# Layer one's gated recurrence run beside the 17 tiles of that layer's projection

## What is computed

```python
xn = rms_norm(h, norm_mix_g[layer])
...
proj = xn @ cd_w_in[j]
lru_x, lru_g, m_x, m_o, m_if = split_cols(proj, CD_SIZES)
...
def rglru_group(xb, gate, conv_w, conv_b, gate_w, gate_b, lam):
    ...
    xc = causal_dwconv(xb.astype(F32), conv_w, conv_b)
    xblk = xc.reshape(B, T, LRU_BLOCKS, LRU_BLOCK)
    gates = jnp.einsum('btnd,gnde->gbtne', xblk, gate_w).reshape(2, B, T, LRU_WIDTH) + gate_b[:, None, None, :]
    r_gate = jax.nn.sigmoid(gates[0])
    i_gate = jax.nn.sigmoid(gates[1])
    log_a = -LRU_C * r_gate * jax.nn.softplus(-lam)
    u = jnp.sqrt(-jnp.expm1(2.0 * log_a)) * (i_gate * xc)
    h = linear_recurrence(jnp.exp(log_a), u)
    return h * jax.nn.gelu(gate.astype(F32))
```

## Time and profile before

| | |
|---|---|
| median of 3 runs | 3634.97 us (3629.35 to 3637.94) |
| the profiled execution | 3619.69 us, its span 3617.7 us |
| PE matmul busy | 3265.8 us (90%) |
| DVE busy | 2353.3 us (65%) |
| ACT busy | 1575.7 us (44%) |
| mean granted clock of TensorE | 0.929 |

### The profile page before, as it was taken

The page is one execution under the profiler, slowest core; times in us unless marked ns, Lnnn a source line. Parts: engine busy times, 40 slices in busy tenths (PEclk is TensorE's granted clock), DMA queues, the critical chain, the costliest instruction groups (busy, mean ns, idle before and its releaser), DMA issues.

```text
span 3617.7 us, 42372 instructions
## 1 busy us (share of the span) xinstructions
PE 3265.8 (90%) x15738; PEld 2681.4 (74%) x15738; DVE 2353.3 (65%) x2345; ACT 1575.7 (44%) x1584; POOL 185.4 (5%) x212
## 2 busy tenths in 40 slices
PE   7967988999999858999998697769999999999996
PEld 6757977878788637878787575658888888888884
DVE  4545436467755446457753436458999999999995
ACT  3131214332223144332222214337777777777772
POOL 0000000000000000000000000000111110111110
PEclk9957988999999978999999897769999999999997
DMA  5200003334433202334432220249999999999993
GB/s 180 82 1 1 1 13 91 104 97 151 145 114 105 76 12 82 99 105 146 144 104 91 92 78 1 82 164 351 387 380 388 379 384 384 381 386 378 390 376 137
DMA packets 118820, 638.42 MB, mean 176 GB/s; under 512 B 13416, under 2 KB 13416, under 8 KB 68784
## 3 DMA queue, kind: packets, MB, share of 16 engines
q1 hardware_dynamic: 98592, 560.52, 41.6%
q0 software_dynamic: 20112, 76.24, 7.0%
HBM read 612.07 MB, written 24.64 MB: 176 GB/s over the span
## 4 chain that ended last, share of the span: by engine, by line
PE 73%; DVE 10%; ACT 2%; issue 1%; DMA 1%; DVEq 1%; SPq 0%; ACTq 0%; POOLq 0%
PE banks L328 25%; PE banks L2467 19%; PE banks L2484 9%; PE banks L920 7%; PE banks L341 3%; DVE chunk_split L301 1%; PE banks L2461 1%; PE banks L2452 1%; PE banks L2473 1%; PE banks L578 1%; PE banks L601 1%; PE banks L1793 1%; DVEq L2769 0%; DVE scratch L1002 0%; DVE scratch L389 0%
## 5 line engine op out<-in xcount | busy, mean ns | idle before, releaser
L328 PE MATMUL banks<-x_scratch,chunk_split 128*128 128x512 f32 x3648 | 845.9, 393 | 36.3 <-DVE x_scratch L315 22.7
L328 PEld LDWEIGHTS banks<-x_scratch,chunk_split 128*128 128x128 f32 x3648 | 686.9, 189 | 189.4 <-issue 46.7
L295 ACT CAST chunk_split<-weight_ring 128x1024 fp32r<-128x1024 f32 x292 | 306.2, 1049 | 987.9 <-PE banks L328 739.9
L2467 PE MATMUL banks<-pair_split,rows 128*128 128x512 f32 x3072 | 710.0, 392 | 0.0
L2467 PEld LDWEIGHTS banks<-pair_split,rows 128*128 128x128 f32 x3072 | 578.6, 188 | 126.5
L301 DVE TENSOR_TENSOR chunk_split<-weight_ring,chunk_split 128x1024 fp32r<-128x1024 f32 x292 | 357.0, 1223 | 227.5 <-ACT chunk_split L295 219.3
L2484 PE MATMUL banks<-pair_split,hidden_t 128*128 128x512 f32 x1536 | 361.4, 394 | 6.1 <-DVE hidden_t L2579 6.1
L2484 PEld LDWEIGHTS banks<-pair_split,hidden_t 128*128 128x128 f32 x1536 | 285.5, 189 | 69.1 <-issue 6.3
L2246 DVE TENSOR_TENSOR pair_split<-mixed,pair_split 128x2048 fp32r<-128x2048 f32 x128 | 293.0, 2290 | 34.5 <-ACT pair_split L2241 34.5
L2246 DVE TENSOR_TENSOR pair_split<-scratch,pair_split 128x2048 fp32r<-128x2048 f32 x128 | 290.4, 2288 | 36.8 <-ACT pair_split L2241 36.7
L2246 DVE TENSOR_TENSOR pair_split<-weight_ring,pair_split 128x2048 fp32r<-128x2048 f32 x128 | 290.3, 2289 | 36.1 <-ACT pair_split L2241 36.1
(11 more groups left out here) (576 smaller groups left out, 3925.3 us busy)
## 6 DMA issues: line engine op xcount, KB each, us to landing
weight_ring<-in_weights SPq DMA_DIRECT2D x292, 512.0 KB, 3.6
mixed<-in_w SPq DMA_DIRECT2D x128, 1024.0 KB, 8.9
weight_ring<-in_w SPq DMA_DIRECT2D x128, 1024.0 KB, 7.6
scratch<-in_w SPq DMA_DIRECT2D x128, 1024.0 KB, 8.7
mixed<-in_w_ada POOLq DMA_DIRECT2D x48, 512.0 KB, 3.8
token_sums<-tables POOLq DMA_DIRECT2D x1, 2560.0 KB, 21.6
residual<-in_x POOLq DMA_DIRECT2D x4, 512.0 KB, 10.0
projected<-in_mem POOLq DMA_DIRECT2D x2, 1024.0 KB, 5.2
```

The lines of the kernel that those rows point to most:

```text
L295: act.copy(chunk_split[:, 0, at:at + KB * P], flat(ring[:, n % RING])).then_inc(chunk_hi.sem, 1)
L328: mm = pe.matmul(lin.bank(j), chunk_split[:, a, at + k * P:at + (k + 1) * P], lin.split[b][k][:, 0:lin.tokens], start=(k, a, b) == (0, 0, ...
L2467: mm = pe.matmul(banks[:, n, :], rows[:, a, k, :], pair_split[k % SLOTS][:, b, n * T:(n + 1) * T], start=False, stop=(k, a) == (KB - 1, 1))
```

## The change

The stage `rg_lru` is gone. Its work is written as a class, `RgLru`, whose three functions are generators: each `yield` ends a piece. `layer_end` gets the object and three numbers (8, 10, 3), and in its loops over the 17 tiles each engine does one piece per tile behind its own work on the tile: PE from tile 8, ACT at tile 3 and from tile 10, DVE from tile 3. What is left of each is done behind the last tile. A bare `yield` lets a tile pass with no piece. The eight gate products are made in two groups of four in banks 4 to 7, which the projection doesn't use; the second group waits until the sigmoids have read the first. The sigmoids are made in two groups of four accordingly. The buffers move to places that are free at that time (PROJ 17 to 25 and XN), and each hand-over has a semaphore of its own. The arithmetic is the same. Line numbers behind L880 differ between the two files.

```diff
--- before.py
+++ after.py
@@ -880,7 +880,7 @@
             if after:
                 aux("lru_gate", (down_started, 1), [(flat(MIX[:, 4:6, :]), d["lru_gate"])])
                 aux("ml_qkv", (down_started, 1), [(small, d["ml_qkv"])])
-                n_next, next_gain_name, next_out = after
+                n_next, next_gain_name, next_out, mixer, pe_from, act_from, dve_from = after
                 next_lin = Linear(n_next, x_split["scratch"])
                 next_gain = [vec(next_gain_name, k) for k in range(KB)]
                 next_norm = RowRoots(T, [S(n)[:, 0, :] for n in range(KB)], S(32)[:, 0, :], 7)
@@ -921,6 +921,7 @@
                                                down.split[b][k], start=(k, a, b) == (0, 0, 0), stop=(k, a) == (FF_TILES - 1, 1))
                         mm.then_inc(chunk_used.sem, 1)
                 if after:
+                    beside = mixer.pe(pe, next_lin.freed)
                     for j in range(next_lin.n):
                         if j < 4:
                             pe.wait_ge(h_ready.sem, h_base + DOWN_BANKS.index((next_lin.f0 + j) % 4) + 1)
@@ -928,6 +929,10 @@
                         if j == 0:
                             pe.wait_ge(h_ready.sem, h_base + DOWN_BANKS.index(next_norm.bank) + 1)
                             sum_squares(pe, next_norm)
+                        if j >= pe_from:
+                            next(beside, None)
+                    for _ in beside:
+                        pass
 
             def act(act):
                 if layer == 0:
@@ -973,12 +978,17 @@
                     if after and g == DOWN_CHUNKS - 1 and m >= 2:
                         next_x(act, m - 2)
                 if after:
+                    beside = mixer.act(act, next_lin.freed)
                     for j in range(next_lin.n):
                         chunk_high(act, next_lin, j)
                         if j < 2:
                             next_x(act, KB - 2 + j)
                         elif j == 2:
                             take_roots(act, next_norm)
+                        if j == 3 or j >= act_from:
+                            next(beside, None)
+                    for _ in beside:
+                        pass
 
             def next_x(act, k):
                 act.wait_ge(h_ready.sem, h_base + k + 1)
@@ -1065,6 +1075,8 @@
                 for k in range(6, KB):
                     add_square(dve, next_norm, k)
 
+                beside = mixer.dve(dve, next_lin.freed)
+
                 def next_tile(j):
                     dve.wait_ge(chunk_used.sem, next_lin.used(j))
                     dve.tensor_tensor(next_out(j), next_lin.bank(j), next_norm.roots, ALU.mult).then_inc(bank_free.sem, 1)
@@ -1075,7 +1087,11 @@
                         invert_roots(dve, next_norm)
                         next_tile(0)
                     next_tile(j - 1)
+                    if j >= dve_from:
+                        next(beside, None)
                 next_tile(next_lin.n - 1)
+                for _ in beside:
+                    pass
 
             stages.append({"pe": pe, "act": act, "dve": dve})
 
@@ -1714,45 +1730,73 @@
             return ins
 
 
-        def rg_lru():
...
-            xc, r, i_gate, th, w, h = S(0, 4), S(4, 4), S(8, 4), S(12, 4), S(16, 4), S(20, 4)
...
-            e, v, dd, eq, sp, neg, pos, ab = (rate[:, n, :] for n in range(8))
...
+        lru_conv, lru_gates, lru_r, lru_i, lru_log = sem("lru_conv"), sem("lru_gates"), sem("lru_r"), sem("lru_i"), sem("lru_log")
+        lru_rate, lru_tanh, lru_w, lru_decay, lru_root = (sem("lru_rate"), sem("lru_tanh"), sem("lru_w"), sem("lru_decay"),
+                                                          sem("lru_root"))
+        lru_gelu, lru_scanned = sem("lru_gelu"), sem("lru_scanned")
+
+        class RgLru:
+
+
+            def __init__(self):
+                self.x, self.g = PROJ[:, 0:4, :], PROJ[:, 4:8, :]
+                self.xc, self.r, self.i_gate, self.th = S(0, 4), S(4, 4), XN[:, 0:4, :], XN[:, 4:8, :]
+                self.w, self.h = PROJ[:, 17:21, :], PROJ[:, 21:25, :]
+                self.gate_w = flat(MIX[:, 4:6, :])
+                rate = PROJ[:, 25, 0:48].rearrange("p (n c) -> p n c", c=4)
+                self.e, self.v, self.dd, self.eq, self.sp, self.neg, self.pos, self.ab = (rate[:, n, :] for n in range(8))
+
+            def pe(self, pe, projected):
                 need(pe, "lru_gate")
-                pe.wait_ge(dve_step.sem, v0 + 3)
-                for n in range(8):
-                    mm = pe.matmul(banks[:, n, :], gate_w[:, n * P:(n + 1) * P], xc[:, n % 4, :], start=True, stop=True)
...
+                pe.wait_ge(lru_conv, 1)
+                for n in range(4):
+                    mm = pe.matmul(banks[:, 4 + n, :], self.gate_w[:, n * P:(n + 1) * P], self.xc[:, n, :], start=True, stop=True)
+                mm.then_inc(lru_gates, 1)
+                yield
+                yield
+                pe.wait_ge(lru_r, 1)
+                for n in range(4):
+                    mm = pe.matmul(banks[:, 4 + n, :], self.gate_w[:, (4 + n) * P:(5 + n) * P], self.xc[:, n, :],
+                                   start=True, stop=True)
+                mm.then_inc(lru_gates, 1)
+
+            def act(self, act, projected):
                 L = link["act"]
...
-                act.wait_ge(pe_step.sem, p0 + 1)
+                L(act.activation(self.ab, vec("lru_lam", 0, 4), ACT.Abs))
+                L(act.activation(self.e, self.ab, ACT.Exp, scale=-1.0))
+                act.activation(self.v, self.e, ACT.Ln, bias=1.0).then_inc(lru_log, 1)
+                yield
+                act.wait_ge(lru_gates, 1)
                 for n in range(4):
...
-                act.wait_ge(dve_step.sem, v0 + 2)
+                    ins = act.activation(self.r[:, n, :], banks[:, 4 + n, :], ACT.Sigmoid, bias=vec("lru_gb", n))
+                ins.then_inc(lru_r, 1)
+                yield
+                act.wait_ge(lru_r, 1)
+                act.wait_ge(lru_rate, 1)
                 for n in range(4):
...
+                    ins = act.activation(self.th[:, n, :], self.r[:, n, :], ACT.Tanh, scale=self.pos[:, n:n + 1])
+                ins.then_inc(lru_tanh, 1)
+                yield
                 for n in range(4):
...
-                act.wait_ge(dve_step.sem, v0 + 4)
...
+                    ins = act.activation(self.r[:, n, :], self.r[:, n, :], ACT.Exp, scale=self.neg[:, n:n + 1])
+                ins.then_inc(lru_decay, 1)
+                yield
+                act.wait_ge(lru_gates, 2)
+                for n in range(4):
+                    ins = act.activation(self.i_gate[:, n, :], banks[:, 4 + n, :], ACT.Sigmoid, bias=vec("lru_gb", 4 + n))
+                ins.then_inc(lru_i, 1)
+                yield
+                yield
+                act.wait_ge(lru_w, 1)
+                act.activation(flat(self.w), flat(self.w), ACT.Sqrt).then_inc(lru_root, 1)
+                yield
+                act.wait_ge(bank_free.sem, projected(7))
+                act.activation(flat(self.g), flat(self.g), ACT.Gelu_apprx_tanh).then_inc(lru_gelu, 1)
+
+            def dve(self, dve, projected):
                 L = link["dve"]
...
+                lam, e, v, dd, eq, sp = vec("lru_lam", 0, 4), self.e, self.v, self.dd, self.eq, self.sp
+                dve.wait_ge(lru_log, 1)
 
                 L(dve.tensor_scalar(dd, e, 1.0, -1.0, ALU.add, ALU.add))
                 L(dve.tensor_scalar(eq, dd, 0.0, None, ALU.is_equal))
@@ -1763,25 +1807,51 @@
                 L(dve.tensor_tensor(eq, eq, e, ALU.mult))
                 L(dve.tensor_tensor(v, v, eq, ALU.add))
                 L(dve.tensor_scalar(sp, lam, -1.0, 0.0, ALU.mult, ALU.max))
...
-                dve.wait_ge(dve_step.sem, v0 + 1)
...
-                conv4(dve, xc, x, "lru").then_inc(dve_step.sem, 1)
-                dve.wait_ge(act_step.sem, a0 + 2)
...
-                dve.wait_ge(act_step.sem, a0 + 4)
...
+                L(dve.tensor_tensor(sp, sp, v, ALU.add))
+                dve.tensor_scalar(self.pos, sp, 8.0, None, ALU.mult)
+                dve.tensor_scalar(self.neg, sp, -8.0, None, ALU.mult).then_inc(lru_rate, 1)
+                yield
+                dve.wait_ge(bank_free.sem, projected(3))
                 for n in range(4):
...
-                dve.wait_ge(dve_step.sem, v0 + 5)
...
-            stages.append({"pe": pe, "act": act, "dve": dve})
+                    ins = dve.tensor_scalar(self.xc[:, n, :], self.x[:, n, :], vec("lru_cw", 12 + n), vec("lru_cb", n),
+                                            ALU.mult, ALU.add)
+                L(ins)
+                yield
+                for back in (1, 2, 3):
+                    for n in range(4):
+                        ins = dve.scalar_tensor_tensor(self.xc[:, n, back:T], self.x[:, n, 0:T - back],
+                                                       vec("lru_cw", 4 * (3 - back) + n), self.xc[:, n, back:T],
+                                                       ALU.mult, ALU.add)
```

(33 more changed lines are left out.)

31 lines of the change are left out of this document (removed).

## The result

The changed kernel takes 3581.28 us (median of 4 runs, 3580.91 to 3582.37) against 3632.16 (4 runs, 3622.43 to 3637.94): ratio 0.9863, 95% interval 0.9840 to 0.9886, so 41 to 58 us less. The forecast was faster, 3596, range 3581 to 3606: the direction is right, and the time is inside the range by 0.3 us at its lower edge. The two profiled executions differ by 3617.7 − 3579.0 = 38.7 us, where the sum said 38.8.

The account below looks back on a forecast made before the run. It took the projection as bound by TensorE and the recurrence by VectorE and ScalarE, on the path. 53.5 − 6.9 − 7.7 was given as 38.8 us less: 3634.97 − 38.8 = 3596, range 3581 to 3606.

Parts of the forecast that it names:

- the sum: Whole change: 53.5 us removed, less 6.9 for gate products and 7.7 left behind the last tile, 38.8 us less.
- The 53.5 us removed: Path from layer one's last projection tile written out (1248.35) to the start of mlstm (1301.82), 53.5 us.
- the 7.7 left: Behind the last projection tile: its write-out, a link, then scans up to the hand-over to mlstm, 7.7 us.
- 2 × 3.43 = 6.9 for the gate products: Eight gate products moved onto TensorE's busy projection, two groups of four at 3.43 us, add 6.9 us.
- Side work hidden in the slots: VectorE and ScalarE pieces within 5.44 us projection tiles, largest VectorE piece 2.75, all ScalarE pieces under 4.3: all hidden.
- the limit of 3.4 us for VectorE: In one projection tile, VectorE has 3.4 us for side work before it makes TensorE wait.
- `mlstm` as it is: The stage behind the recurrence was taken as unchanged in length, 78 us, leaving the gain at 38.8 us.
- the bounds of 0.9 lost to 2.5 gained: mlstm's query products: wholly at half clock 0.9 us lost, wholly at full clock 2.5 us more gained.
- 3596 as a median: Whole kernel: median of three runs, 3634.97, less 38.8 gives 3596 us; the forecast had 82 in 100.
- 15 us of spread: The profiled execution of the kernel before showed that the same program can take 15 us less than the median.
- Rival (c): TensorE's clock falls in the projection; with all 17 tiles at half clock 54 us slower, 3689; 2 in 100.

Follow-up runs that it names:

- e6: The changed kernel with six of its eight gate products left out; median 3583.9 us, ratio 0.9867.
- e5: The changed kernel with two of the convolution's accumulations in one VectorE slot and one slot left free; median 3597.9 us, ratio 0.9912.
- e9: The changed kernel with pieces drawn together before the last tile, plus 11 extra products between mlstm's value and query products; median 3577.3 us, ratio 0.9850.
- e11: The kernel of e9 with six extra fp32 products ahead of layer zero's rwkv_scan; 3579.0 us, ratio 0.9853.
- e2: The changed kernel again, unedited, on the same chip as runs of the kernel before; 3593.46 us (6 runs), ratio 0.9905.

## Why the prediction was right, and what was off

- **The 53.5 us removed and the 7.7 left**: 53.47 and 7.65 in the traces. Right. (The terms as the forecast gives them add up to 38.9, not 38.8; the piece measured 38.77.)
- **2 × 3.43 = 6.9 for the gate products**: from tile 2's cast, which waits for tile 0's products (1160.46, now 1158.84), to the last write-out (1248.35, now 1253.78) are 87.89 and 94.94 us, 7.05 more. e6 shows 0.86 a product. Right, 0.15 short.
- **Side work hidden in the slots**: no wait of TensorE in the changed kernel; the limit of 3.4 us for VectorE held from both sides, by the conv slots (2.73 fit, 0.84 to spare) and e5 (5.49 overran by 2.11, 2.1 expected). Right. ScalarE's slots held too: a table load takes 1.28 us, and the exponentials begin at 1220.00, 0.02 behind the load at 1218.70. The Trainium skill, "ScalarE: Activation LUTs", section "What ACT_TABLE_LOAD costs", counts about 2.66 us for a change of set, a drain included; this trace agrees on the load and disagrees on the drain, which none of the seven loads of the new stage shows.
- **`mlstm` as it is**: wrong by 2.6 us, outside the bounds of 0.9 lost to 2.5 gained. The step that failed is the bound: it took the query products as the only ones whose clock could change. They lost 0.57, within it; the picks, columns and first scores behind them lost more (0.9, 1.5, 0.5), and the last group gained 0.9. What the forecast quoted of the Trainium skill, "TensorE: Matmul & The Clock Gate", section "What's actually happening", a count of slow products that differs from run to run, is neither borne out nor refuted: the length repeated between two executions of each kernel (the table of the starts), while e9 and e11 differ by 5.5 us with the same instructions. The direction of the whole was not touched. That the profiled pair came out at 38.7 all the same is luck: the pieces ahead (1.6 us) and behind (0.9), which the change doesn't touch, made up for it.
- **3596 as a median**: the sum was subtracted from a median of runs which, by their times, mostly had the scan at 0.50; the four runs of the result lie where the profiled execution lay, at the lower edge (3580.9 + 0.4), and e2's at 3593.5. The range held, by 0.3 us, because its lower end was taken from the profiled execution: the size of the term is confirmed by the traces and by e2, not by the median of the result. Of what the forecast called 15 us of spread, 12.8 is layer zero's scan at 0.50 or at 1.00.
- **Rival (c)**: did not come. What the forecast quotes there of the Trainium skill, "TensorE: Matmul & The Clock Gate", section "A second HAM failure mode: psum-queue depth-cycling", speaks of short idles between the groups. The projection has hardly any (88.3 of 89 us busy before, 93.67 of 95.20 after), so its granted clock of 1.00 doesn't disagree with that section, as the forecast says; it only lacks the condition.

## What to carry to other kernels

Work of two idle engines is hidden in a matmul-bound loop if each piece is shorter than the slot less what the loop itself has on that engine; the slack is read from one slot of the timeline, and the gain of that piece is then a subtraction that held to a few tenths of a us here. The stage behind it can still change its length, by 2.6 us here. Keep a margin: in e5 a stall of 2 us cost 4, since the clock fell with it. Where two kernels' medians differ from what their traces say, cut both traces at the same instructions first and see whether the difference lies in the part that was changed.

## What the runs showed of the hardware

- A stage of small products (64 columns, a link to VectorE per step) started at a granted clock of 1.00 behind 1.57 us of idle in all eleven profiles without extra products there; in some the clock then fell to 0.50 within 2 us and stayed there to the stage's end, in others of the same program it stayed at 1.00. The stage took 42.20 or 29.41 us.
- One idle of 2.11 us between dense products was followed by a granted clock of 0.52 over the next 3 us; the projection of the changed kernel, without that idle, stayed at 1.00.
- The length of `mlstm` repeated to 0.1 us over two executions of the kernel before and two of the changed one, and differed by 5.5 us (75.9 and 81.4) between e9 and e11, which are the same from layer zero's scan on but for e11's six products at its start.
